# A latent-attention block's output projection in 3 + 5 chunks, with half of the first block inside the last head's slots

## The reference

```python
c_q = rms_norm(x @ w_dq, q_norm_g)
q = (c_q @ w_uq).reshape(B, S, N_HEADS, QK_NOPE_DIM + QK_ROPE_DIM)
...
k_nope = (c_kv @ w_uk).reshape(B, S, N_HEADS, QK_NOPE_DIM)
v = (c_kv @ w_uv).reshape(B, S, N_HEADS, V_HEAD_DIM)
...
p = jax.nn.softmax(s * scale, axis=-1).astype(v.dtype)
return jnp.einsum('bhqk,bkhd->bqhd', p, v)
...
return o @ w_o
```

## Time and profile before

| what | us |
|---|---|
| median of 3 runs | 2746.73 (2746.29 to 2749.33) |
| span of the profiled execution, first to last instruction | 2743.8 |
| the median beyond that span | 2.9 |
| PE matmul busy | 2665.3 (97%) |
| POOL / DVE / ACT busy | 1613.6 / 1423.0 / 986.2 |
| chain that ended last, by engine | PE 80%, DVE 11%, POOL 5% |

### The profile page before, as it was taken

How to read it: one execution, slowest core, us unless ns; L and a number is a source line. 1 busy time by engine, 2 the same in 40 slices (tenths; PEclk the granted TensorE clock), 3 DMA queues, 4 the chain that set the end, 5 groups by cost and what they waited for, 6 DMA issues and landing times.

```text
span 2743.8 us, 36352 instructions
## 1 busy us (share of the span) xinstructions
PE 2665.3 (97%) x14266; PEld 2460.2 (90%) x14266; DVE 1423.0 (52%) x2553; ACT 986.2 (36%) x1647; POOL 1613.6 (59%) x874
## 2 busy tenths in 40 slices
PE   7999999999899999999999999999899999999998
PEld 7899999888678899999898999998899788999998
DVE  5643333669967643333664433337766476433335
ACT  4232332446543232332432322334445242323323
POOL 2576776669733576776636866674211234768665
PEclk9999999999999999999999999999999999999999
DMA  3222221311012222221421212232000111212213
GB/s 136 74 68 71 83 77 47 138 62 47 31 39 77 85 70 70 85 76 48 161 85 62 77 54 70 77 128 77 9 24 30 71 77 69 78 62 77 80 59 123
DMA packets 55464, 201.45 MB, mean 73 GB/s; under 512 B 6144, under 2 KB 6656, under 8 KB 55296
## 3 DMA queue, kind: packets, MB, share of 16 engines
q1 hardware_dynamic: 49248, 177.12, 19.5%
q10 hardware_dynamic: 6048, 22.02, 2.1%
HBM read 186.53 MB, written 12.58 MB: 73 GB/s over the span
## 4 chain that ended last, share of the span: by engine, by line
PE 80%; DVE 11%; POOL 5%; issue 3%; ACT 2%; DMA 0%; SPq 0%; POOLq 0%; DVEq 0%; ACTq 0%
PE ps L958 26%; PE ps L959 26%; PE ps L960 26%; POOL pacc L945 4%; DVE raw_sum L1625 2%; POOL w_lo L905 1%; DVE sum L1625 1%; DVE x L1643 1%; PE ps L1058 1%; DVE y L1632 1%; DVE y L1649 1%; PE ps L1194 1%; DVE pair L1523 0%; DVE xn L1696 0%; ACT w_hi L1252 0%
## 5 line engine op out<-in xcount | busy, mean ns | idle before, releaser
L905 POOL TENSOR_TENSOR w_lo<-w_stage,w_hi 128x1024 fp32r<-128x1024 f32 (+1 forms) x455 | 1019.3, 2268 | 576.1 <-ACT w_hi L1252 570.1
L958 PE MATMUL ps<-xn,w_hi 128*128 128x384 f32 x1920 | 646.9, 337 | 5.7 <-issue 4.2
L959 PE MATMUL ps<-xn,w_hi 128*128 128x384 f32 x1920 | 643.3, 335 | 0.0
L960 PE MATMUL ps<-xn,w_lo 128*128 128x384 f32 x1920 | 642.9, 335 | 0.0
L1252 ACT ACTIVATE w_hi<-w_stage 128x1024 fp32r<-128x1024 f32 (+1 forms) x455 | 436.5, 983 | 79.2 <-POOL w_stage L916 55.0
L958 PE MATMUL ps<-w_hi,hid 128*128 128x512 f32 x1056 | 412.7, 391 | 4.9 <-DVE y L1637 3.4
L960 PE MATMUL ps<-w_hi,hid 128*128 128x512 f32 x1056 | 411.4, 390 | 0.0
L959 PE MATMUL ps<-w_lo,hid 128*128 128x512 f32 x1056 | 411.3, 390 | 0.0
L958 PEld LDWEIGHTS ps<-xn,w_hi 128*128 128x128 f32 x1920 | 361.5, 188 | 9.5 <-issue 7.8
L959 PEld LDWEIGHTS ps<-xn,w_hi 128*128 128x128 f32 x1920 | 361.6, 188 | 1.7
L960 PEld LDWEIGHTS ps<-xn,w_lo 128*128 128x128 f32 x1920 | 361.3, 188 | 0.0
(11 more groups left out here) (196 smaller groups left out, 4034.1 us busy)
## 6 DMA issues: line engine op xcount, KB each, us to landing
w_stage<-weights SPq DMA_DIRECT2D x311, 512.0 KB, 3.6
x_kept<-x ACTq DMA_DIRECT2D x18, 512.0 KB, 2.6
x<-x_kept ACTq DMA_DIRECT2D x18, 512.0 KB, 7.0
g_pre<-rows SPq DMA_DIRECT2D x7, 512.0 KB, 5.3
x<-x_in SPq DMA_DIRECT2D x6, 512.0 KB, 7.9
g_post<-rows SPq DMA_DIRECT2D x6, 512.0 KB, 5.5
x<-x_in ACTq DMA_DIRECT2D x6, 512.0 KB, 8.0
y_out<-x SPq DMA_DIRECT2D x5, 512.0 KB, 2.6
```

Of the source, the lines that this page charges most:

```text
L905: pool.tensor_tensor(w_lo[:, s, 0:n], w_stage[:, s, 0:n], w_hi[:, s, 0:n].bitcast(F32), ALU.subtract).then_inc(w_split, 1)
L958: pe.matmul(out, a[0], m[0], start=start, stop=False)
L959: pe.matmul(out, a[0], m[1], start=False, stop=False)
L960: return pe.matmul(out, a[1], m[0], start=False, stop=stop)
```

## The change

The attention block's projection is cut in 3 + 5 chunks in place of 4 + 4 (HEAD_BLOCKS). Of the twelve items of the first block, six stand in the slots 42 to 47 of the last head, two in the two slots behind them that finish the softmax, one ahead of the last value product, and three follow it. Their banks are 2 and 3, which the projections used. The last head's keys and values no longer go to slots 4 to 6, but over the low parts of the latent queries and into `act_out`, so units 349, 350 and 351 are freed at the end of the seventh head ("attention", 21), and only 352 at the end of attention; `g_pre` is loaded in front of 352. The first block frees 345, 346 and 347; the second frees 348 to 352. PE waits for the second block's weights chunk by chunk.

```diff
+HEAD_BLOCKS = ((0, 3), (3, 5))
...
-    return FFN_BLOCKS if SUBS[b] == "ffn" else ROW_BLOCKS
+    return {"ffn": FFN_BLOCKS, "conv": ROW_BLOCKS, "mla": HEAD_BLOCKS}[SUBS[b]]
...
-def out_bank(last, j):
-    return LAST_BANKS[j] if last else 4 + j % 2
+def out_bank(b, last, j):
+    return LAST_BANKS[j] if last else (2 if SUBS[b] == "mla" else 4) + j % 2
...
+            early = iter([(t, h) for t in range(TILES) for h in range(2)])
+
+            def early_down():
+                t, h = next(early)
+                down(b, 0, t, h, 2 * t + h)
+
             for n in range(QK + 2):
...
                 if 1 <= n <= QK:
                     s.add(0, "divide", n - 1)
+                if n >= QK - 6:
+                    early_down()
                 if n >= 2:
                     s.add(0.4, "probs_turn", n - 2)
                 if n >= 5 and n % 2 == 1:
                     s.add(0.6, "value", (n - 5) // 2)
+                    if n == 5 + 2 * (3 * (HEADS - 1) - 1):
+                        for i in range(4, 7):
+                            s.free(UNIT0[b] + i, "attention", 3 * (HEADS - 1))
                 s.weights()
+            early_down()
             s.add(0.6, "value", QK // 2 - 1)
-            for i in range(4, 8):
-                s.free(UNIT0[b] + i, "attention", QK // 2)
-            s.weights(until=row_unit(b, 3))
-            for t in range(TILES):
-                for h in range(2):
-                    down(b, 0, t, h, 2 * t + h)
+            s.free(UNIT0[b] + 7, "attention", QK // 2)
+            for t, h in early:
+                down(b, 0, t, h, 2 * t + h)
             s.weights(until=row_unit(b, 7))
             last_down(b)
...
+        last_kn = over("last_kn", [P, 2, TOK], spot["y"] + LAT * TOK * 4, F32R)
+        last_val = [over("last_val_hi", [P, TILES, VDIM], spot["y"] + (LAT + 2) * TOK * 4, F32R),
+                    over("last_val_lo", [P, TILES, VDIM], spot["act_out"], F32R)]
...
-                if u == row_unit(4, 4):
+                if u == row_unit(4, 7):
                     row(g_pre[:, :], PRE_ROW + 5, pre_loaded)
...
-                elif j == 0:
+                elif j == 0 and SUBS[b] == "conv":
                     pe.wait_ge(w_split, row_unit(b, c0 + nc_ - 1) + 1)
+                if SUBS[b] == "mla" and n == 0 and j == 0:
+                    pe.wait_ge(proj_done, 6 * HEADS)
...
                 for k in range(nc_):
+                    if SUBS[b] == "mla" and j == 0:
+                        pe.wait_ge(w_split, row_unit(b, c0 + k) + 1)
```

More of the change, by code:

```diff
@@ L781, in qr, with keys_of, values_of @@
             return xn[rows_, i, h + 1, cols_] if h + 1 < HEADS else qr7[i][rows_, cols_]
+        def keys_of(h, i):
+            return last_kn[:, i, :] if h == HEADS - 1 else kn[:, h % 2, i, :]
+        def values_of(h, i):
+            return last_val[i][:, :, :] if h == HEADS - 1 else val[:, h % 2, i, :, :]
         def own_rows(h):
@@ L1043, in down @@
                         src, w = both(xn, c0 + k, toks(t)), unit(row_unit(b, c0 + k), h * WIDE, WIDE)
-                    mm = mm3(ps[:, out_bank(last, j), :], src, w, k == 0, k == nc_ - 1)
+                    mm = mm3(ps[:, out_bank(b, last, j), :], src, w, k == 0, k == nc_ - 1)
                 mm.then_inc(out_full, 1)
@@ L1183, in score @@
                 mm3(out, [qn[:, h % 2, i, toks(t)] for i in range(2)],
-                    [kn[:, h % 2, i, ks] for i in range(2)], True, False)
+                    [keys_of(h, i)[:, ks] for i in range(2)], True, False)
                 mm3(out, [qr(h, i, slice(0, P), toks(t)) for i in range(2)], [lat[:, i, LAT - 1, ks] for i in range(2)],
@@ L1206, in value @@
                 for k in range(nk // P):
-                    mm = mm3(ps[:, 6 + j % 2, 0:2 * P], [val[:, h % 2, i, k0 // P + k, :] for i in range(2)],
+                    mm = mm3(ps[:, 6 + j % 2, 0:2 * P], [values_of(h, i)[:, k0 // P + k, :] for i in range(2)],
                              [pt[j % 2][i][:, k, :] for i in range(2)], k == 0, k == nk // P - 1)
@@ L1403, in proj @@
                 elif i < 4:
-                    to, src = kn[:, h % 2, 0, cols(i - 2)], ps[:, bank, 0:HALF]
+                    to, src = keys_of(h, 0)[:, cols(i - 2)], ps[:, bank, 0:HALF]
                 else:
                     t0, nt = (0, 4) if i == 4 else (4, 2)
-                    to = val[:, h % 2, 0, t0:t0 + nt, :]
+                    to = values_of(h, 0)[:, t0:t0 + nt, :]
                     src = ps[:, bank, 0:nt * P].rearrange("p (a n) -> p a n", a=nt)
@@ L1628, in down @@
                 last = n == len(blocks(b)) - 1
-                src, dst = ps[:, out_bank(last, j), :], y[:, t, half_row(h)]
+                src, dst = ps[:, out_bank(b, last, j), :], y[:, t, half_row(h)]
                 dve.wait_ge(out_full, d + 1)
@@ L1836, in proj @@
                 elif i < 4:
-                    to, src = [kn[:, h % 2, j, cols(i - 2)] for j in range(2)], ps[:, bank, 0:HALF]
+                    to, src = [keys_of(h, j)[:, cols(i - 2)] for j in range(2)], ps[:, bank, 0:HALF]
                 else:
                     t0, nt = (0, 4) if i == 4 else (4, 2)
-                    to = [val[:, h % 2, j, t0:t0 + nt, :] for j in range(2)]
+                    to = [values_of(h, j)[:, t0:t0 + nt, :] for j in range(2)]
                     src = ps[:, bank, 0:nt * P].rearrange("p (a n) -> p a n", a=nt)
```

## The result

| | before | after |
|---|---|---|
| median of the comparison's runs, us | 2749.33 (2746.29 to 2754.44) | 2758.87 (2756.70 to 2760.35) |
| span of the profiled execution, us | 2743.8 | 2758.3 |

The ratio is 1.0035, with a 95% interval of 1.0024 to 1.0046. The kernel became slower by 9.6 us (6.6 to 12.6). The traced execution of after took 2760.35 us, the longest of its five. The prediction had +6.5 us. Its direction, its likeliest case and the list of places were right. Its size was too small, and the median lies 1.2 us above its range.

A forecast was written before the change was run, and what follows sets the result against it. TensorE (PE), busy for 97% of the span, was taken as the bound. Terms -6.4 - 6.6 + 0.5 + 15.6 = +3.1 us, with the clock +6.5, took the 2746.7 us median to 2753.2; range 2747.5 to 2757.7.

The forecast's parts named there:

- Last head, -6.4: Last head's slots: nine early items cover PE's waits for DVE's scaling of the probabilities, giving 6.4 us back.
- The half-filled slots: Rival in the last head: ACT or DVE comes to bound a slot, slots fill only by half; +3.2 us, 2756.4, chance 0.12.
- the hold of DVE's scalings: Rival in the last head: POOL's added splits hold DVE's scalings without cover; +5.5 us on the forecast, 2758.7, chance 0.1.
- Second block, -6.6: Projection's second block: PE's work grows from 35.2 to 43.4 us, DVE's norm chain fits under it; 6.6 us gained.
- Unit 352, +0.5: Projection: the last unit loads after attention and is ready at 9.3 us against PE's 8.8; wait 0.5 us, bounds 0 and 1.5.
- The loss in the opening: Last FFN's opening: later splits make PE wait 8.6, 3.5 and 3.5 us, 15.6 together, plus 3.4 for the clock.
- The first wait, 8.6 us: Last FFN's opening: PE waits 8.6 us for unit 356's split after the first up item, which ends at E + 8.4.
- PE may go on at E + 17.0: Last FFN's opening: 356's split ends 16.8 us behind DVE's last add, itself at E + 0.15; E is the projection matmuls' end.
- The clock, 3.4 us: Behind the opening's waits: two falls of PE's clock at 1.7 us each, 3.4 us; bounds 1.7 and 5.1.
- of the two 3.5 us waits I count one: Last FFN's opening: beside the 8.6 us wait, only one of the two 3.5 us waits brings a clock fall, 1.7 us each.
- No fall of the clock (0.2): Rival in the last FFN's opening: waits as forecast but the clock stays up; +3.1 us, 2749.8, chance 0.2.
- The faster rival (0.08): Rival in the opening: 355 and 356 rounded ahead of the first Silu, one 3.7 us wait, one fall; -7.1 us, 2739.6, chance 0.08.

The follow-up runs named there:

- e2: The changed kernel without early items: all twelve items of the first block behind the last value product; +15.1 us against before (11.5 to 18.7).
- e5: The kernel before with only the late places of units 355 to 360 in the written order, loads as early as before; +18.7 us against before.
- e6: e3 with slots 2 and 3 exchanged for the last FFN's second chunk, so unit 355 loads early; -9.6 us against before, 2739.5 us.
- e1: The kernel before with unit 348's slot counted free only at the projection's end (the late-release kernel); +16.2 us against before (12.4 to 20.1).
- e8: e6 with the splits of units 357 and 358 also ahead of the first Silu, and 360's moved up; -7.1 us against before, median 2740.1.
- e3: The changed kernel with splits of 355 and 356 ahead of the first Silu, 357 behind it, 358 to 360 around the second; -7.1 us against before.
- e7: e4 with unit 348's split written into slot 43 in place of slot 45; -5.2 us against before (-7.7 to -3.0).
- e4: The changed kernel with 4 + 4 chunks and early items of four chunks from slot 45 on; +3.0 us against before (0.3 to 5.8).

## Why the prediction was right, and where it was off

**Last head, -6.4: right.** The stretch is full and the early items are worth 6.1 us by the traces of after and e2, which differ only in them. The half-filled slots and the hold of DVE's scalings, rivals with 0.12 and 0.1, did not come: PE has no wait in the 35.2 us.

**Second block, -6.6: right in size, the reason only in part.** Measured -6.8 (e2). The prediction gave all of it to PE's longer work. By e5 4.2 us come with 4 + 4 chunks as well, when the splits of 355 and 356 leave the block, and the prediction moved these splits without asking what their leaving gives. That the number holds all the same is in part luck. For the longer work speaks e6: unit 355 is split in the second block there, and PE has no wait in it. **Unit 352, +0.5: right.** PE's wait for it is 0.3 us.

**The loss in the opening: right in kind, place and number, too small in size.** It was put at 15.6 us of waits and 3.4 for the clock, 19.0. It is 23.6. Two terms were mis-sized, the clock by 2.8 us and the first wait by 2.2.

- *The first wait, 8.6 us, measured 10.8* (2222.30, where the last matmul's share ends, to 2233.10). The step that failed is "PE may go on at E + 17.0". The times were read from the earlier trace rows, where DVE was on time. In before the norm's `x` step on DVE started 0.30 us ahead of POOL's split (rows below). Both chains have one length in before, after, e1 and e2: DVE's step comes 10.07 us behind its last add, POOL's split 10.1 to 10.2 us behind the start of the first `up` item. Before, that item started 0.18 us behind the add, by the 0.39 us wait of the earlier trace rows. After, the wait is gone and it starts 0.20 us ahead of the add (2213.95 and 2214.15). So POOL's split came first, and DVE's step took 3.36 us, 2.1 more than its 1.28, all of it in the chain to unit 356. The late-release kernel still has the 0.39 us wait, keeps DVE first, and goes on 16.7 us behind the first item's start by its own trace, where after needs 19.15: 2.1 us of hold, and 0.4 because the item starts earlier against DVE's add. The prediction had both facts, that the add would move to E + 0.15 and what a split does to DVE, and didn't put them together.
- *The clock, 3.4 us, measured 6.2* (23.6 less 17.4 of waits, their modelled ends counted). The step that failed is "of the two 3.5 us waits I count one": it fell behind all three waits. The outer bound of 5.1 was too low as well, since it took each fall to last 3.3 us at the lower level; the third went on for twice that. One wait was counted out on the 3.01 us wait of the earlier trace rows, and the trace of before didn't support such odds. Beside the 3.02 and 2.60 us of the earlier trace rows it has four more waits of this size, 4.20, 4.57, 2.92 and 2.97 us (at 729.32, 750.59, 761.08 and 1965.21), with the lower clock right behind each. So six paid and one didn't, and "over twice any wait behind which the clock fell" is wrong too: twice 4.57 is more than 8.6.

The rows of before behind the first point, DVE's step and POOL's split, and the clock behind the 2.97 us wait for the second:

```profile
2232.95 1.28 DVE L1643 SCALAR_TENSOR_TENSOR x<-y,pair,x 128x1024 f32<-128x1024 f32 x1
2233.25 3.24 POOL L905 TENSOR_TENSOR w_lo<-w_stage,w_hi 128x1024 fp32r<-128x1024 f32 x1 [2.94 <-ACT w_hi L1252]
1965.80:1969.10 3.30, 3.30 (x12) 3.30 (x11) 2.58 (x6) 1.73 (x4) 0.00 (x0) 0.50 0.00 0
```

The prediction weighed the Trainium skill's section on HAM oscillation (TensorE: Matmul & The Clock Gate), by which all three waits would pay, and chose against it. The trace of after agrees with that rule. Falls stand behind shorter waits too: 1.9 us in e6 and 2.4 in e8.

The page SBUF — State Buffer of the Trainium skill, section "SBUF: two separate sides", says that VectorE and GpSimd share one port pair as an exclusive lock, for VectorE where an operation has two inputs in SBUF or runs in a 2-port mode: whichever operation starts first keeps it for its whole length. The traces agree: the same two operations, VectorE's with two large inputs in SBUF, took 3.36 and 2.42 us with POOL ahead by 0.14 us, and 1.28 and 3.19 with DVE ahead by 0.30.

**No fall of the clock (0.2): wrong.** **The faster rival (0.08):** its condition, roundings ahead of the first Silu, was not met by the change, and met by hand it gave its number (e3), by parts that fit: one wait of 3.8 us for 3.7, POOL through both splits 12.3 us behind the first item's start for 12.

**Sum.** -12.9 + 17.4 + 6.2 = +10.7 on the traces; the medians say +9.6. The predicted +6.5 lies just below the interval's 6.6. The kernel before itself took 2749.3 us in this comparison, 2.6 more than in the runs that the prediction started from; +9.6 on those gives 2756.3, inside the range and 3 us above the forecast.

What stays open: each fall's length is read, not explained. That the hold of DVE costs 2.1 us of the time is shown in the chain of two kernels with it (after, e2_chunks_only) and two without (e1_late_release, e5_late_places); no kernel removed the hold alone from after. How the second block's 6.8 us divide between the longer work and the two splits that left is bounded by e5, not measured in after. Why some of the traced executions start their first weight matmul 2.3 us later is not known.

## What to carry to other kernels

When a buffer's release moves behind a block, follow not only the load that waits for it but the place that the planner gives to everything queued behind it: here the load cost nothing, the places in the written order cost some 17 to 19 us in the kernel before (e5, by the traces and by the times), and two lines that moved them made the changed kernel 7 us faster than before, not 10 slower. When times are read from a trace to price a new chain, ask of each neighbour on a shared resource which of the two starts first, since a few tenths of a microsecond can decide who pays. And before a fall of the clock is counted out on one wait that was free, list every wait of that size in the trace: here six had paid.

## What the runs showed of the hardware that was not expected

- The hold between DVE and POOL doesn't scale with the size of the held operation: a 128 x 2 operation of 0.16 us took 2.28 to 2.33 us beside a split of 2.4 us (e8), and four of them in a row, beside four splits (9.4 us), each took as long as one. The 128 x 1024 step of 1.28 us lost about as much, 2.1 us. So a norm chain of many small steps loses more beside a row of splits than one large step does.
- After the three waits of after, 10.8, 3.4 and 3.4 us, the granted clock stayed low for some 3.7, 3.1 and 6.2 us in which PE was busy, so two waits of one length cost 1.5 and 3.1 us.
- The length of one wait doesn't settle whether the clock falls. It fell behind waits of 1.9 and 2.4 us (e6, e8). The same 3.01 us wait for DVE's norm step was followed by the lower clock in e7, and not in before and e4:

```profile
2202.20:2205.50 3.30, 3.30 (x10) 2.65 (x9) 3.14 (x9) 2.89 (x7) 2.40 (x1) 0.50 0.03 12
2207.10:2210.50 3.40, 3.40 (x20) 2.93 (x21) 3.37 (x6) 2.13 (x5) 2.27 (x1) 1.00 0.00 0
```

The first row is e7's, the second e4's. In e1 the clock also fell in the last head, behind a 1.9 us wait that before and e5 have without a fall.
